# A recurrent stage in 64-token chunks: every chunk product as 64x64 tiles on compact buffers, and the next block's set-up issued inside the present block's chunk steps

## What is computed

```python
def rwkv7_time_mix(h, mu, w_r, w_k, w_v, w_o, ...):
    ...
    r_, k_, v_, a_ = heads(r), heads(k), heads(v), heads(a)
    decay = jnp.exp(-jnp.exp(heads(w)))

    def step(state, inp):
        r_t, d_t, k_t, v_t, kk_t, a_t = inp
        sa = jnp.einsum('bhij,bhj->bhi', state, -kk_t)
        state = (state * d_t[:, :, None, :] + sa[..., None] * (kk_t * a_t)[:, :, None, :]
                 + v_t[..., None] * k_t[:, :, None, :])
        return state, jnp.einsum('bhij,bhj->bhi', state, r_t)
    ...
    _, y = lax.scan(step, jnp.zeros((b, RWKV_HEADS, RWKV_HEAD_DIM, RWKV_HEAD_DIM), f32), xs)
```

## Time and profile before

| | us |
|---|---|
| median of 3 executions | 2934.71 |
| the three executions | 2939.19, 2934.71, 2934.19 |
| span of the profiled execution, first to last instruction | 2937.1 |
| TensorE busy in it | 2777.1 (95%) |
| VectorE, ScalarE, GpSimd busy | 1286.8, 1121.8, 127.8 |
| blocks 0 to 3 of the time mix, in the trace | 999.67 to 1246.83 |

### The profile page before, as it was taken

One profiled execution on the slowest core, in us unless ns is written; L12 is line 12 of the kernel. 1 busy time (PEld: TensorE's weight loads), 2 busy tenths in 40 slices (PEclk: granted clock), 3 DMA queues, 4 the chain that ended last, 5 costly groups with the idle time before them and its releaser, 6 DMA issues.

```text
span 2937.1 us, 44160 instructions
## 1 busy us (share of the span) xinstructions
PE 2777.1 (95%) x18364; PEld 2190.7 (75%) x18364; DVE 1286.8 (44%) x2139; ACT 1121.8 (38%) x2023; POOL 127.8 (4%) x129
## 2 busy tenths in 40 slices
PE   8989889999999999999999999999899999999998
PEld 6879657887877887878797666666598876666665
DVE  5456257545547744665465122221286451122212
ACT  5454236445446422364453222222364342222222
POOL 0000000000000121200010000000001300000000
PEclk9999889999999999999999999999999999999999
DMA  8524657545435211064344899999742048999996
GB/s 333 200 103 173 263 223 271 204 170 213 176 127 192 96 58 58 30 229 183 118 174 170 334 418 417 415 416 417 321 146 85 1 158 330 416 417 413 418 415 256
DMA packets 96403, 701.55 MB, mean 239 GB/s; under 512 B 10688, under 2 KB 10816, under 8 KB 11328
## 3 DMA queue, kind: packets, MB, share of 16 engines
q1 hardware_dynamic: 96192, 698.59, 59.9%
HBM read 697.50 MB, written 1.05 MB: 238 GB/s over the span
## 4 chain that ended last, share of the span: by engine, by line
PE 89%; DVE 5%; ACT 3%; issue 2%; DMA 1%; SPq 0%; DVEq 0%; ACTq 0%
PE bank L1589 15%; PE bank L826 12%; PE bank L828 12%; PE bank L827 12%; PE bank L1649 8%; PE bank L1567 4%; PE bank L1676 4%; PE bank L1927 2%; PE bank L1935 2%; PE bank L1939 2%; PE bank L2601 1%; PE bank L1458 1%; PE bank L1461 1%; PE bank L1473 1%; DMA weight_ring<-weight_slots 1%
## 5 line engine op out<-in xcount | busy, mean ns | idle before, releaser
L1589 PE MATMUL bank<-weight_ring,packed_h 128*64 128x256 f32 x2176 | 285.4, 379 | 0.0
L826 PE MATMUL bank<-source_hi_lo,weight_hi_lo 128*128 128x256 f32 x864 | 252.2, 292 | 12.7 <-DVE source_hi_lo L816 8.9
L1589 PE MATMUL bank<-more_slots,packed_h 128*64 128x256 f32 x1920 | 257.0, 379 | 1.5 <-ACT packed_h L1576 1.5
L826 PE MATMUL bank<-gate_up_hi_lo,x_hi_lo 128*128 128x512 f32 x640 | 253.2, 396 | 1.4 <-DVE gate_up_hi_lo L944 1.4
L1589 PEld LDWEIGHTS bank<-weight_ring,packed_h 128*64 128x64 f32 x2176 | 196.4, 137 | 74.3 <-issue 18.1
L828 PE MATMUL bank<-gate_up_hi_lo,x_hi_lo 128*128 128x512 f32 x640 | 249.8, 390 | 0.0
L827 PE MATMUL bank<-gate_up_hi_lo,x_hi_lo 128*128 128x512 f32 x640 | 249.3, 390 | 0.0
L827 PE MATMUL bank<-source_hi_lo,weight_hi_lo 128*128 128x256 f32 x864 | 247.0, 286 | 0.0
L828 PE MATMUL bank<-source_hi_lo,weight_hi_lo 128*128 128x256 f32 x864 | 246.7, 286 | 0.0
L1589 PEld LDWEIGHTS bank<-more_slots,packed_h 128*64 128x64 f32 x1920 | 174.0, 137 | 69.7 <-issue 15.4
L785 DVE TENSOR_TENSOR weight_hi_lo<-weight_ring,weight_hi_lo 128x1024 fp32r<-128x1024 f32 x141 | 171.8, 1222 | 87.6 <-ACT weight_hi_lo L779 87.3
(11 more groups left out here) (569 smaller groups left out, 5329.4 us busy)
## 6 DMA issues: line engine op xcount, KB each, us to landing
weight_ring<-weight_slots SPq DMA_DIRECT2D x443, 1024.0 KB, 7.5
more_slots<-weight_slots SPq DMA_DIRECT2D x212, 1024.0 KB, 9.1
params_sb<-small_params SPq DMA_DIRECT2D x1, 3196.5 KB, 18.6
h_sb<-weight_slots SPq DMA_DIRECT2D x3, 1024.0 KB, 5.9
y_sb<-weight_slots SPq DMA_DIRECT2D x3, 1024.0 KB, 8.0
x_sb<-x_by_tokens SPq DMA_DIRECT2D x1, 1024.0 KB, 4.8
out_by_tokens<-x_sb SPq DMA_DIRECT2D x4, 256.0 KB, 2.2
params_sb<-small_params SPq DMA_DIRECT2D x1, 70.5 KB, 4.6
```

Of the source, the lines that this page charges most:

```text
L826: e.matmul(out, w[0], x[0], start=start, stop=False, skip_group_check=shared)
L1589: mm = e.matmul(ps[x * CAP:(x + 1) * CAP, m * FB:(m + 1) * FB], self.hc[:, c, (2 * (p % 2) + x) * CAP:(2 * (p % 2) + x + 1) * CAP], wt[:, ...
```

## The change

All products inside a block become 64x64 tiles: contraction over 64 partitions, 64 weight columns, 64 moving columns. The buffers hold only the diagonal 64x64 pieces (`[P, n, 4, 64]`: the upper 64 partitions are chunk 0 of the block, the lower 64 are chunk 1). Class ChunkInverse takes the place of Inverse in this stage, with T and its transpose in one buffer. The masked operand of a product is kept in two buffers (`z`, block parity), so that the set-up of block it + 1 can be issued in pieces inside the chunk steps of block it (`READY`). VectorE masks 512 columns that hold two products at once, GpSimd's copies of U, the zeroed halves and the copies of V and R into them are gone, VectorE copies U of the second head, and y is made chunk by chunk. R of the last block is kept aside by one GpSimd copy (`R_kept`). The masks in the parameters change: 2 of 128 columns go, 9 of 64 come. The scratch area of the program is set to 8192 bytes by an argument of the constructor.

```diff
--- before.py
+++ after.py
...
+def chunked(ps, lo=0, m=4):
+    return ps[:, lo:lo + m * 64].rearrange("p (m t) -> p m t", m=m)
+
+
+def each(mask, m=4):
+    return mask.unsqueeze(1).to_broadcast([P, m, 64])
...
+class ChunkInverse:
...
+    def product(self, e, ps, lo, left, right):
+
+        for m in range(4):
+            for i in range(2):
+                rows = slice(64 * i, 64 * i + 64)
+                mm = e.matmul(ps[rows, lo + 64 * m:lo + 64 * m + 64], left(rows, m), right(rows, m), start=True, stop=True)
+        return mm
...
+        ps = k.banks.take(e, self.key("xt", l), ("inv_sum", *self.key(l)))
+        e.wait_ge(*k.ge("inv_x", *self.key(l)))
+        mm = self.product(e, ps, 0, x, tt)
+        if not last:
+            mm = self.product(e, ps, 256, tt, x)
+        mm.then_inc(*k.up("inv_products", *self.key(l)))
...
+            T_ = b["T"][:, :, :, :].rearrange("p a m t -> p (a m) t")
+            m = 4 if last else 8
+            e.tensor_tensor(T_[:, 0:m, :], T_[:, 0:m, :], chunked(k.banks.at(*self.key("xt", l)), 0, m), ALU.add).then_inc(*k.up("inv_sum", *self.key(l)))
...
+    PIECES = ("V", "A", "B", "R", "K", "lv")
+    READY = {(0, 1): ("A",), (0, 2): ("V",), (1, 0): ("B",), (1, 1): ("R",), (1, 2): ("K", "lv")}
...
+        else:
+            ps = [k.banks.take(e, (n, "masked", piece, it, par), ("masked", n, it, par, piece)) for par in range(2)]
+            right = self.sg if piece == "A" else self.r
+            for x, left in enumerate((self.a, self.kk_)):
+                for m in range(4):
+                    for i in range(2):
+                        cols, c = self.cut(it, i), 64 * (4 * x + m)
+                        for par in range(2):
+                            f = slice(64 * par, 64 * par + 64)
+                            mm = e.matmul(ps[par][64 * i:64 * i + 64, c:c + 64], left[f, self.ch(it, m), cols], right[f, self.ch(it, m), cols], start=True, stop=True)
...
```

395 lines of the change are left out of this document (217 added, 178 removed).

## The result

The changed kernel takes 2848.8 us, the median of 4 runs (2840.9 to 2851.5); the kernel before took 2934.7 beside it (4 runs). The ratio is 0.9705, with a 95% interval of [0.9694, 0.9717]: 86 us or 3% less, where 2844 was forecast.

A forecast was written before the change was run, and what follows sets the result against it. TensorE was taken to bound the stage; its four blocks fall from 247.2 to 156.4 us (-90.8), larger masks add 0.5, so 2934.7 - 90.3 = 2844 us. Range 2826 to 2918; the forecast's own 2826 to 2868, chance 0.66.

The forecast's parts named there:

- the chain: In a level of one inverse: products, ScalarE's copy, products, VectorE's addition, with hand-offs, one after another: 3.34 us.
- The record of 64x64: TensorE's 64x64 products: 0.031 us per record when neighbours use other quarters of the array, bounds 0.024 and 0.056.
- rival A: Quarters do not run side by side, as diagonal products write one bank: 0.056 us a record, 2918 us; chance 0.14.
- Masked products: In a block's set-up: 128 masked records at 0.031 us each, 5.0 us together with 32 LakV records.
- The level: One level of a block's two inverses: 3.35 us, for 5.58 before.
- The inverse: In each block: start 1.27 us, four levels of 3.35, last level 2.3; 17.0 us, for 29.0 before.
- The blocks: Blocks 0 to 3 of the stage: 41.2, 34.9, 43.6 and 36.7 us, 156.4 for 247.2 before.
- The last chunk: Block 3's last chunk step: W stands on VectorE behind two weight splits and four gate operations, 3.7 us of waiting.
- the signs: What the trace after should show, among it a TensorE wait of 2 to 3 us in block 3's final chunk step.
- rival B: TensorE's clock falls to 1.2 GHz in the stage: 0.062 us a record, 2964 us; chance 0.05.
- C: A third of the stage at low clock, or waits between small products: +25 to +55 us, 2870 to 2900; chance 0.12.
- Every later stage as long as before: Expected in the trace after: from the first product with w_o on, no stage changes its length.

The follow-up runs named there:

- the edit that shortened one link alone: Changed kernel with VectorE's addition of a level made in two halves, the transpose first, each with a signal: 2845.0 us, ratio 0.9698.
- The one profile that left no wait there: Changed kernel with halved addition, one weight slot a level and a new order of block 3's last chunk step: 2838.3 us, ratio 0.9673.

## Why the prediction was right

Its time was 2844 and the measured one 2848.8, by the mechanism that it gave: quarters of the array side by side until the chain bounds a level. That the sum came so near is in part luck, since sizes inside it were off in both directions. Step by step:

- **The record of 64x64**: forecast 0.031 us, measured 0.029 for diagonal pairs. That they write one bank did not matter, so rival A falls. The Trainium skill's rule ("TensorEngine Tiling (Array Packing)", Restrictions and Gotchas), by which row tiles cannot use the same PSUM bank at once, does not agree with 16 records in 0.47 us here, in one bank but in other partitions of it; the measurement decides.
- **Masked products** were mis-sized, at 0.031 for 0.0156: block 0's head took 6.2 us for 8.1, its chunk steps 14.2 (1019.74 to 1033.94) for 16.1. I had rows for two quarters only and did not think of four. By the "issue floor" of about 25 ns in the Trainium skill ("TensorE: Matmul & The Clock Gate", Back-to-back issue gap), which makes no difference between products in one quarter and in four, 64 records would have taken 1.6 us by my estimate; they took 1.0, so the trace disagrees.
- **The level**: forecast 3.35, measured 3.42, bound by the chain as said; the edit that shortened one link alone brought 3.15.
- **The inverse**: forecast 17.0, measured 18.3 in block 0 (1001.51 to 1019.8). The last level took 2.9 us for my 2.3, one other 3.86.
- **The blocks**: 41.2, 34.9, 43.6, 36.7 forecast; 38.6, 37.6, 40.8, 35.5 measured, 152.5 in all for 156.4. The errors had both signs and cancel in part, which is luck. Block 1's is the pause: with the slots spread the block takes 34.9. The forecast had said that the weights have room in this stage, and for the weights that was so; it had not asked what else is held up while they are in flight.
- **The last chunk** was mis-sized too: a wait of 3.7 us in the sum (2 to 3 in the signs), 1.27 measured. W stood behind the splits and the gate operations as foreseen, but TensorE's gate product ran beside them. What I had left out is behind it: the low clock of the last 3 us and the first 8 of the next stage, and 1.40 us for the copy of y.
- **The clock** (rival B) stayed at 1.00 in the levels in spite of a gap of 0.25 us in each. In the first profile it stayed full behind the pause of block 1 also; in the three others of the same program it fell to 1.2 GHz there, for 3 to 7 us. Each stretch of low clock in the stage begins beside a wait, the shortest of 0.60 us; behind other waits as long it stayed full. C had its waits in the right form, but 4 us of them.
- **Every later stage as long as before** holds within 1 us for their sum in the profile of after. In the three repeats of that program the rest took 1696.6, 1695.7 and 1691.4 us for 1690.3 before. What makes it longer there was not followed up.
- **The 5 us between 2844 and the median.** The four profiled executions of the changed program took 2840.9, 2850.7, 2849.9 and 2852.3 us, on average 90.7 less than the profiled one of before (2939.2), where the sum gave 90.3. By parts, on average: the stage gave back 92.4 us (245.8 before, from the first masked product; 153.4) for the forecast 90.8, it began 1.5 us earlier, and the rest took 3.4 us longer. But the execution of before from which all prices were read was 4.5 us above its own median; where it spent them no second trace of before can say, and that is what separates 2844 from 2848.8.

## What to carry to other kernels

Where TensorE is the bound and its products hold zeros beside a diagonal, split them over quarters of the array. The chain, and no longer the number of records, may then set the time: compute it hand-off by hand-off, as here, where it was right to 2%. When a stage gets three times as many instructions per us, look at what is in flight on the DMA engines beside it, and try asking for weights one at a time there. In a stage's last step, ask for each engine what stands ahead of the one operation that TensorE waits for; and when you move it, what stands behind it now.

## What the runs showed of the hardware

- 64x64 fp32 records in four quarters start 64 to the us (0.0156 us), in two diagonal quarters 0.029, in the one quarter of the U products 0.059 to 0.062 (from the first start to the sixteenth 0.88 and 0.93 us in block 0).
- Four products of one quarter (eight records) followed by four of the other still start 26 to 34 records to the us: a record of a free quarter started at 1013.07, ahead of three that stand before it in the program (1013.13 to 1013.24).
- With four slots of 1 MB in flight TensorE stopped for 2.66 to 2.93 us in four profiles of the changed program, always at the same product; with the slots spread over four levels, in two profiles, for 0.46 and 0.35 us there and 0.59 and 1.20 a level later; with the slots 12 us later for 0.19 there.
- Behind a wait of 1.27 us in the last chunk, with one of 1.40 us 5 us later, the clock was at 1.2 GHz for some 10 us. The one profile that left no wait there kept 2.4 GHz, and kept it behind a wait of 2.43 us as well, so a wait does not always bring the clock down.
